# A third row buffer for the last but one expert pair, and two row-number loads begun together

## The reference, cut to what matters

```python
for g in range(N_EXPERT_GROUPS):
    sl = slice(g * EXPERTS_PER_GROUP, (g + 1) * EXPERTS_PER_GROUP)
    hid = jax.nn.silu(jnp.einsum('md,edf->mef', x, w_gate[sl])) * jnp.einsum('md,edf->mef', x, w_up[sl])
    wg = jnp.where((g_sel == g)[:, None], comb, 0.0).astype(x.dtype)
    y = y + jnp.einsum('mef,me,efd->md', hid, wg, w_down[sl])
```

## Time and profile before

| what | us |
|---|---|
| median of 3 runs | 962.42 |
| the 3 runs, lowest and highest | 960.98, 966.94 |
| the profiled execution, its own time | 960.92 |
| its span in the trace, first to last instruction | 959.1 |

### The profile page before, as it was taken

One profiled execution on the slowest core, in us unless ns is written; L12 is line 12 of the kernel. 1 busy time (PEld: TensorE's weight loads), 2 busy tenths in 40 slices (PEclk: granted clock), 3 DMA queues, 4 the chain that ended last, 5 costly groups with the idle time before them and its releaser, 6 DMA issues.

```text
span 959.1 us, 12358 instructions
## 1 busy us (share of the span) xinstructions
PE 828.2 (86%) x4741; PEld 591.0 (62%) x4741; DVE 474.1 (49%) x1074; ACT 263.4 (27%) x650; POOL 199.1 (21%) x172
## 2 busy tenths in 40 slices
PE   5999898999989896999999899989899987976910
PEld 5997798989878794788888644587333332322300
DVE  5998365757576668885136324372131101010158
ACT  4221443434354247574412111111011101010100
POOL 2664424242103361110000000004211111011000
PEclk9999899999998797999999999979999999896965
DMA  8320211111043122573622193276999999999152
GB/s 312 88 90 18 82 45 44 45 45 45 1 187 114 52 97 91 217 245 131 243 110 88 47 429 138 67 287 222 351 422 424 423 425 419 424 426 374 51 190 87
DMA packets 34474, 182.15 MB, mean 190 GB/s; under 512 B 10996, under 2 KB 11652, under 8 KB 23857
## 3 DMA queue, kind: packets, MB, share of 16 engines
q1 hardware_dynamic: 25488, 159.24, 42.6%
q0 software_dynamic: 7744, 17.86, 5.3%
q10 hardware_dynamic: 1184, 4.26, 1.1%
HBM read 169.03 MB, written 20.77 MB: 198 GB/s over the span
## 4 chain that ended last, share of the span: by engine, by line
PE 59%; DVE 19%; DMA 14%; issue 3%; POOL 1%; ACT 1%; SPq 1%; POOLq 0%; DVEq 0%; ACTq 0%
PE bank L584 10%; PE bank L585 9%; PE bank L586 9%; DMA y_f<-in_w_gu 8%; PE bank L1017 7%; PE bank L577 6%; DVE r_f L1479 6%; PE bank L1026 4%; DMA x_f<-scr_id 2%; PE bank L768 2%; PE bank L674 1%; PE bank L800 1%; DMA small_f<-scr_h,x_f 1%; PE bank L708 1%; PE bank L799 1%
## 5 line engine op out<-in xcount | busy, mean ns | idle before, releaser
L1017 PE MATMUL bank<-x_f,r_f 128*64 128x512 f32 x272 | 126.9, 622 | 9.8 <-DMA y_f<-in_w_gu 9.0
L584 PE MATMUL bank<-r_r,w_r 128*128 128x268 f32 x416 | 126.0, 303 | 10.7 <-DVE w_r L1456 10.1
L585 PE MATMUL bank<-y_r,w_r 128*128 128x268 f32 x416 | 122.7, 295 | 0.0
L586 PE MATMUL bank<-r_r,w_r 128*128 128x268 f32 x416 | 122.7, 295 | 0.0
L585 PE MATMUL bank<-w_r,r_r 128*128 128x512 f32 x240 | 96.3, 401 | 0.0
L584 PEld LDWEIGHTS bank<-r_r,w_r 128*128 128x128 f32 x416 | 82.3, 198 | 15.6 <-DVE w_r L1456 10.1
L584 PE MATMUL bank<-x_r,r_r 128*128 128x512 f32 x200 | 81.8, 409 | 3.9 <-DVE w_r L1763 3.8
L585 PEld LDWEIGHTS bank<-y_r,w_r 128*128 128x128 f32 x416 | 82.4, 198 | 0.0
L586 PEld LDWEIGHTS bank<-r_r,w_r 128*128 128x128 f32 x416 | 82.2, 198 | 0.0
L586 PE MATMUL bank<-x_r,w_r 128*128 128x512 f32 x200 | 80.4, 402 | 0.0
L1017 PEld LDWEIGHTS bank<-x_f,r_f 128*64 128x64 f32 x272 | 38.3, 143 | 63.0 <-issue 63.0
(11 more groups left out here) (371 smaller groups left out, 1552.2 us busy)
## 6 DMA issues: line engine op xcount, KB each, us to landing
x_f<-in_w_gu SPq DMA_DIRECT2D x17, 2048.0 KB, 29.6
w_f<-in_w_d SPq DMA_DIRECT2D x22, 1024.0 KB, 29.7
y_f<-in_w_gu SPq DMA_DIRECT2D x10, 2048.0 KB, 28.0
w_f<-in_w_f SPq DMA_DIRECT2D x26, 512.0 KB, 3.7
w_f<-in_w_gu SPq DMA_DIRECT2D x6, 2048.0 KB, 23.0
x_f<-in_w_d SPq DMA_DIRECT2D x11, 1024.0 KB, 33.5
w_f<-in_w_t SPq DMA_DIRECT2D x5, 2048.0 KB, 8.1
y_f<-in_state POOLq DMA_DIRECT2D x8, 512.0 KB, 4.7
```

The source lines that it names most:

```text
L584: pe.matmul(out, ah, bh, start=start, stop=False)
L585: pe.matmul(out, ah, bl, start=False, stop=False)
L586: return pe.matmul(out, al, bh, start=False, stop=stop)
L1017: ins = pe.matmul(out[half, :], XT[:, k, half], wgu[s][:, k, :], start=(k == 0), stop=(k == KC - 1))
```

## The change

`X` gets a third buffer `X[2]`, 1024 columns that lie over constants of the routing stage which are no longer read once the tables are made (semaphore `rt_dv` at 4). Pair 14 uses it, with a semaphore of its own, `xs_in2`. POOL clears it and gathers pair 14's rows in the branch of b = 11, right behind the gather of pair 13 and ahead of the scatter of pair 11; the gather of pair 14 behind the loop is gone. PE waits for pair 14's rows as for other pairs. In the loop POOL issues both loads of row numbers one behind the other and waits for both; the gather of the next block's rows comes behind that wait.

```diff
-        X, XT = [cut(R1, D), cut(C1, D)], cut(R1 + D, KC, P)
+        X, XT = [cut(R1, D), cut(C1, D), cut(P, D)], cut(R1 + D, KC, P)
...
         def x_buffer(b):
-            return (b + b // FIRST) % 2
+            return 2 if b == FIRST + 1 else (b + b // FIRST) % 2
...
-                if b == FIRST + 1:
-                    pe.wait_ge(S["ex_in"], x_reloaded)
-                else:
-                    pe.wait_ge(S[f"xs_in{i}"], 16 * sum(x_buffer(c) == i for c in range(N_HOT, b + 1)))
+                pe.wait_ge(S[f"xs_in{i}"], 16 * sum(x_buffer(c) == i for c in range(N_HOT, b + 1)))
                 turn_x(X[i], "xtr_mm")
...
-            x_reloaded = pe.snap(extras * 16 + 32)
...
                     elif b == FIRST - 2:
                         gather_pair(FIRST, f"xs_in{x_buffer(FIRST)}")
+                        p.wait_ge(S["rt_dv"], 4)
+                        p.memset(X[2], 0.0).then_inc(S["none_pl"], 1)
+                        p.wait_ge(S["none_pl"], 3)
+                        gather_pair(FIRST + 1, f"xs_in{x_buffer(FIRST + 1)}")
                 scatter_pair(b)
...
                             id_column[bass.ds(j + (NE + 1), 1)].rearrange("e r o -> r e o"),
                             allow_slow_non_contiguous=True).then_inc(S["tb_in"], 16)
-                p.wait_ge(S["tb_in"], j * 32 + 48)
-                gather(X[1][0:CAP, :], extra_at[0][0:CAP, :], "ex_in", p.snap(bounds[0] + 1))
                 p.wait_ge(S["yw_out1"], j * 16 + before)
                 p.dma_start(extra_at[1][0:CAP, :].rearrange("p (e o) -> p e o", e=1),
                             id_column[bass.ds(j + NE, 1)].rearrange("e r o -> r e o"),
                             allow_slow_non_contiguous=True).then_inc(S["tb_in"], 16)
                 p.wait_ge(S["tb_in"], j * 32 + 64)
+                gather(X[1][0:CAP, :], extra_at[0][0:CAP, :], "ex_in", p.snap(bounds[0] + 1))
                 p.wait_ge(S["ex_ac"], j * 3 + 3)
                 p.wait_ge(S["ex_dv"], j * 4 + 4)
                 scatter(extra_at[1][0:CAP, :], Yout[1][0:CAP, :], "yw_out1", p.snap(bounds[1] + 2))
                 p.wait_ge(S["ex_in"], j * 16 + 32)
-            gather_pair(FIRST + 1, "ex_in")
```

More of the change, by code:

```diff
@@ L332, in build @@
                      "none_pl id_out hot_dv rt_dv rt_ac rk_mm h1_out tb_in "
-                     "xs_in0 xs_in1 xtr_mm xt_ev gu_mm sg_ac hid_dv "
+                     "xs_in0 xs_in1 xs_in2 xtr_mm xt_ev gu_mm sg_ac hid_dv "
                      "htr_mm hte_dv dn_mm y_ev ex_mm ex_ac ex_dv ex_in yw_out0 yw_out1 "
```

## The result

The changed kernel took 956.02 us (median of 5 runs, 954.11 to 956.54) against 962.42 before: 6.4 us less. The ratio estimated from all runs is 0.9925, with a 95% interval of 0.9906 to 0.9944. Run again, its median was 955.01 against 963.74, 8.7 us less, a ratio of 0.9903 (0.9875 to 0.9931). The forecast was 953.9, 8.5 us less, a ratio of 0.9911, which both intervals hold.

What follows compares the result with a forecast made beforehand. Pair 14's late rows were taken to bound the last three pairs. The 9.5 us ceiling, cut by expert 31's weights to 8.55 with other terms at 0, gave 962.42 - 8.5 = 953.9 us, range 951.4 to 958.5.

Steps and rivals of the forecast that it cites:

- The hole and what replaces it: Ahead of pair 14's transposes: 7.3 us idle and 2.2 us clock loss vanish; expert 31's weights leave about 1 us wait.
- Cost taken: 0: Pair 14's early gather: at most 0.35 MB, 0.85 us of weight bandwidth, no delay to expert 31's weights; bound 0.5 us.
- Both loads together: POOL's loop: row-number loads issued together bring pair 15's gather to 867.5 to 870; worth 0, securing 3 to 6 us slack.
- Rival 1: At gate_up(14): expert 31's weights land a microsecond earlier, so the full 9.5 us are gained, 952.9; chance 0.15.
- Rival 2: At gate_up(14): weights 2 us later, PE idles about 2.5 us and the clock falls; gain 3.9 us, 958.5; chance 0.13.
- Rival 3: Ahead of down(14): both loads slow each other, pair 15's rows come late, 0 to 2 us lost, 954 to 956; chance 0.05.
- Rival 4: Weight queue: the gather holds it up for its whole flight, 11.55 us; 1.9 us slower, 964.3; chance 0.04.
- Rival 5: POOL's queue: something holds pair 14's early gather beyond 870, so no gain, 962.4; chance 0.01.

Runs made afterwards that it cites:

- e4: Changed kernel with 40 small matmuls keeping PE busy ahead of gate_up(13); last scatter 256.56 us after the common start, against 256.44 in the changed kernel.
- e7: Changed kernel with half of the down weights left out for experts 24, 25, 28 and 29; last scatter at 251.80 us, 4.6 us earlier than in the changed kernel.
- e3: Changed kernel without pair 14's gather, PE multiplying the cleared buffer instead; last scatter at 255.25 us, against 256.44 in the changed kernel.
- e5: Changed kernel with pair 14's early gather made twice; last scatter at 259.00 us, against 256.44 in the changed kernel.
- e8: Kernel before the change, run again unaltered; last scatter at 263.75 us after the common start, wait for pair 14's rows 6.92 us.
- e9: Kernel before the change, run a third time unaltered; last scatter at 264.22 us after the common start, wait for pair 14's rows 10.18 us.
- e1: Third buffer and early gather alone, the loop left as in the kernel before; ratio 0.9917 (0.9894 to 0.9941).

## Why the prediction was right, and where it was off

**The hole and what replaces it: right.** The rows of pair 14 bound the last pairs; with them early PE goes on at once, the clock doesn't fall, and the weights of expert 31 become the next limit. A wait of about 1 us was forecast ahead of gate_up(14), and 1.17 us measured. That these agree so closely is luck in part: the weights of 31 landed 1.1 us later than assumed (R+229.65 against 228.54), and PE reached pair 14's transposes 0.7 us later (R+223.01; the forecast's 873.8 is R+222.28). With PE left as it was, the other runs with one early gather waited 1.34 to 1.88 us. e4 and e7 show that the weights bind and not PE.

**The early gather: mis-sized.** This is the term "Cost taken: 0". By the earlier trace rows I gave it at most 0.35 MB, as half of what two gathers moved; an even half is no upper bound, and it is 0.40 MB. More important was the argument that the weights of 31 don't move, because the gather's bytes leave their way later on. They moved by the gather's price: 1.1 us (e3, after, e5). The load took 42.14 us, not 41.1. Only some 0.2 us was given back, because the late gather of the kernel before had cost the weights of 31 little: there they landed at R+228.54, 228.87 and 228.73 (before, e8, e9), against 228.47 with no gather of pair 14 at all (e3) and 229.14 to 229.77 with an early one. POOL's queue moved 0.60 MB from the issue of the late gather to the landing of 31, and pair 15's gather was in flight too. Why bytes so close ahead of the landing cost it less than the same bytes earlier is open. With 1.1 us for 0, the forecast of 8.5 becomes 7.4, which is what the profiled executions show from R, and 7.6 by the means of three runs of before and five with one early gather. That the forecast's 953.9 lies inside both intervals doesn't bear out the 0: the two medians gained 6.4 and 8.7 us, and 8.5 and 7.4 both lie between.

**Both loads together: right in the result.** Worth 0 on the path. The loop's end came at R+216.88 (pair 15's gather) against 217.53 with the loads apart (e1); the forecast of 867.5 to 870 holds when the 2.5 us are taken off 870.87. The slack is there without it: pair 15's rows landed 7.3 us ahead of their use in e1, with 9.7 in the changed kernel.

**The rivals.** Rival 1 (the weights don't bind): no; the wait is there in every run. Rival 2 (a longer wait, and the clock falls): not in the changed kernel, but e5 is this case, made by one more gather; its wait was 1.3 to 2 us longer than those of the runs with one and PE left as it was. The length alone doesn't decide it, as e4 shows (last section). Rival 3 (pair 15's rows late): no wait in any run. Rival 4 (a gather holds the weights for its whole flight): a gather costs 1.1 us where its flight is over 10, so no. Rival 5: the gather left at 833.15.

**Not tried**: why the gather costs 1.1 us where its bytes take 0.97. The packet counts above don't say: POOL's queue shows 196 more packets with one gather than with none, and only 26 more with two, at the same cost.

## What to carry to other kernels

When a stall is removed, look up when the next input lands, and forecast the gain from there rather than from the stall's length: here 7.2 us of hole and 2.2 us of clock were worth 7.4 together, because the weights stood 1 us behind and the early gather put them back by another 1.1. Where a queue is full from start to end of a stage, moving a transfer to an earlier place in it doesn't hide it: in both early places that were tried, 150 us apart, its bytes delayed the weights that were waited for behind it by the same amount. Where the kernel before had it, issued 10.6 us ahead of their landing, it cost them little. And a load begun early gains little if the next wait in the same queue of instructions has about the same length.

## What I had not expected of the hardware

Two idle times of the same length had different ends: after 3.10 us (e4) the next matmul took 0.61 us, at the full clock, after 3.14 us (e5) it took 1.08. In both PE had worked for over 12 us with no gap above 0.52 us. The wait ahead of gate_up(13) does the same in two executions of the kernel before: after 2.32 us the next matmul took 1.09 us, after 2.33 us (e9) 0.61. What makes the difference wasn't tried. A gather of the next block's rows, of which there are none, still made POOL wait 6.11 us in the changed kernel, and two loads of 64 numbers each made it wait 10.26 us, all with the weight queue full.
